# Grid attention: the value products on the tensor array's column halves, with later turns and products

## The reference, cut to what matters

```
s = q @ k.T / 8 (+ a mask: latent tokens see context, and latents at most 128 away)
p = exp(s - m) / (sum(exp(s - m)) + exp(sink - m))      m: a row maximum
o = p @ v;  y = o @ w_o
```

## Time and profile before

| | us |
|---|---|
| median of the runs | 2492.74 |
| the profiled execution | 2491.8 |
| its span | 2490.2 |
| TensorE busy | 2313.0 (93%) |
| VectorE busy | 1218.8 (49%) |
| ScalarE busy | 971.6 (39%) |
| GpSimd busy | 509.9 (20%) |

### The profile page before, as it was taken

How to read it: one execution, slowest core, us unless ns; L and a number is a source line. 1 busy time by engine, 2 the same in 40 slices (tenths; PEclk the granted TensorE clock), 3 DMA queues, 4 the chain that set the end, 5 groups by cost and what they waited for, 6 DMA issues and landing times.

```text
span 2490.2 us, 37770 instructions
## 1 busy us (share of the span) xinstructions
PE 2313.0 (93%) x16663; PEld 2103.8 (84%) x16663; DVE 1218.8 (49%) x1517; ACT 971.6 (39%) x1153; POOL 509.9 (20%) x453
## 2 busy tenths in 40 slices
PE   6999999989999998889999899979999989888998
PEld 6998889879999997567999877867888877667997
DVE  5645566656555553445555355362133264445444
ACT  3433344444433342334444344333222233534442
POOL 2112434312211111220221111012202210230220
PEclk9999999999999998779999999989999999999999
DMA  6555434355555555676554310113332222213551
GB/s 243 176 173 174 140 119 136 124 198 173 183 178 183 182 176 185 212 253 226 181 186 153 110 35 18 35 68 102 101 102 90 97 97 85 68 51 98 179 182 68
DMA packets 205245, 344.72 MB, mean 138 GB/s; under 512 B 8845, under 2 KB 69498, under 8 KB 205082
## 3 DMA queue, kind: packets, MB, share of 16 engines
q1 hardware_dynamic: 205082, 342.31, 41.5%
HBM read 341.24 MB, written 1.05 MB: 137 GB/s over the span
## 4 chain that ended last, share of the span: by engine, by line
PE 77%; DVE 10%; POOL 6%; ACT 4%; issue 3%; SPq 0%; DMA 0%; DVEq 0%; POOLq 0%; ACTq 0%
PE PS L467 74%; PE PS L476 3%; DVE WL L453 3%; POOL small L1504 1%; ACT WH L440 1%; POOL small L1502 1%; POOL TMP L1513 1%; DVE rstd L588 1%; DVE XL L635 1%; DVE TMP L1430 1%; DVE small L1408 0%; DVE XL L1003 0%; DVE al L999 0%; POOL TMP L1514 0%; DVE TMP L1435 0%
## 5 line engine op out<-in xcount | busy, mean ns | idle before, releaser
L453 DVE TENSOR_TENSOR WL<-raw,WH 128x2048 fp32r<-128x2048 f32 (+2 forms) x281 | 651.5, 2331 | 724.5 <-ACT WH L440 724.5
L467 PE MATMUL PS<-XH,WH 128*128 128x256 f32 (+1 forms) x2336 | 699.6, 299 | 40.3 <-issue 15.3
L467 PE MATMUL PS<-XL,WH 128*128 128x256 f32 (+1 forms) x2336 | 693.5, 297 | 0.0
L467 PE MATMUL PS<-XH,WL 128*128 128x256 f32 (+1 forms) x2336 | 693.3, 297 | 0.0
L440 ACT ACTIVATE WH<-raw 128x2048 fp32r<-128x2048 f32 (+2 forms) x281 | 518.8, 1858 | 360.5 <-PE PS L467 360.0
L467 PEld LDWEIGHTS PS<-XH,WH 128*128 128x128 f32 x2336 | 452.1, 194 | 56.8 <-issue 18.5
L467 PEld LDWEIGHTS PS<-XL,WH 128*128 128x128 f32 x2336 | 453.0, 194 | 10.1
L467 PEld LDWEIGHTS PS<-XH,WL 128*128 128x128 f32 x2336 | 452.8, 194 | 10.0
L467 PE MATMUL PS<-WH,XH 128*128 128x256 f32 (+2 forms) x944 | 287.8, 305 | 19.3 <-DVE XL L635 8.3
L467 PE MATMUL PS<-WH,XL 128*128 128x256 f32 (+2 forms) x944 | 279.3, 296 | 0.0
L467 PE MATMUL PS<-WL,XH 128*128 128x256 f32 (+2 forms) x944 | 279.2, 296 | 0.0
(11 more groups left out here) (236 smaller groups left out, 2574.0 us busy)
## 6 DMA issues: line engine op xcount, KB each, us to landing
raw<-in_ffn_w_in SPq DMA_DIRECT2D x88, 1024.0 KB, 5.1
raw<-in_w_mod SPq DMA_DIRECT2D x48, 1024.0 KB, 5.2
raw<-in_ffn_w_out SPq DMA_DIRECT2D x40, 1024.0 KB, 4.9
raw<-in_a_w_in SPq DMA_DIRECT2D x36, 1024.0 KB, 4.9
raw<-in_w_mlp_in SPq DMA_DIRECT2D x32, 1024.0 KB, 5.5
raw<-in_w_mlp_out SPq DMA_DIRECT2D x32, 1024.0 KB, 5.0
raw<-in_gla_w_in SPq DMA_DIRECT2D x12, 1024.0 KB, 5.1
raw<-in_attn_w_qkv SPq DMA_DIRECT2D x6, 1024.0 KB, 5.0
```

The costliest lines, as they stand in the source:

```text
L453: dve.e.tensor_tensor(self.WL[j % NRAW][:, 0:nk * nn], self.raw[j % NRAW][:, 0:nk * nn], wh.bitcast(F32), ALU.subtract).then_inc(*self.lo. ...
L467: return self.pe.e.matmul(out, l, r, start=start, stop=stop, skip_group_check=skip)
```

## The change

The products swap their operands: 64 columns of values are the weights and the turned probabilities stream; the even head goes to PSUM partitions 0 to 63, the odd one to 64 to 127, their matmuls in turn. `cO` then has the channels on the partitions, as the output products want them. The denominators are spread over 64 columns each by ScalarE (`recips`), transposed by TensorE (`sums`) and multiplied in by VectorE (`out`), after ScalarE copied bank 7 (`out`). The sink is no column of the tile any more: its exponential is made once for a group and segment and added to the sums. Score tiles are 6 instead of 4. Probabilities are turned two double steps after their scores, products made three after. On ScalarE the copy of the turned probabilities stands ahead of both exponentials, on VectorE the negation is made once for both heads. The splits for the output products are made in the last group's double steps.

```diff
+        self.cSM += [v(H, 11280, [128, 512]), v(self.tmp_at, 3072, [128, 512]), self.std, self.rstd]
+        self.cO = v(H, 7184, [128, 4096]).rearrange("p (h k t) -> p h k t", h=2, k=KT)
+        self.cRD = v(self.tmp_at, 3584, [128, 512])
...
+        def pv(g, i0):
...
             for k in range(n):
-                m = self.mm(PS[:, 7, o * 256 + hd * 64:o * 256 + hd * 64 + 64], self.cPT[i % 2][:, k * 128:k * 128 + 128], self.cV[:, k, g * 64:g * 64 + 64], k == 0, k == n - 1)
+                for j in range(2):
+                    m = self.mm(PS[64 * j:64 * j + 64, 7, pair * 256 + o * 128:pair * 256 + o * 128 + 128], self.cV[:, k, g * 64:g * 64 + 64], self.cPT[j][:, k * 128:k * 128 + 128], k == 0, k == n - 1, True)
...
+            if i0 % 8 == 6:
+                self.empties([7], (self.evac, ("grid", "o", g, seg)))
+                sums(g, seg)
+
+        def sums(g, seg):
+            nonlocal spare
+            b = spare = self.GRID_SPARE[spare]
+            pe.wait_ge(self.evac, ("grid", "r", g, seg))
+            self.pe_bank(b)
+            for pair in range(2):
+                for o in range(2):
+                    m = self.tr(PS[:, b, pair * 256 + o * 128:pair * 256 + o * 128 + 128], self.cRD[:, 256 * o + 128 * pair:256 * o + 128 * pair + 128])
...
+            self.empties([b], (self.o_done, ("grid", g, seg)))
...
-        for n in range(34):
+        for n in range(35):
             g, p = divmod(n, 8)
             if n < 32:
...
                 scores(g, 2 * p)
                 next(nxt, None)
-            for j in range(2):
-                if n > 1:
-                    g, p = divmod(n - 2, 8)
-                    pv(g, 2 * p + j)
-                if 1 <= n < 33:
-                    g, p = divmod(n - 1, 8)
+            if n > 2:
+                g, p = divmod(n - 3, 8)
+                pv(g, 2 * p)
+            if 2 <= n < 34:
+                g, p = divmod(n - 2, 8)
+                for j in range(2):
                     turn_p(g, 2 * p + j)
-        for h in range(2):
-            self.turn_o_pe(f"go{h}", self.cO[:, 2 * h:2 * h + 2, :], (self.o_done, ("grid", 3, 1)), h)
...
+            if i % 8 == 7:
+                act.wait_ge(self.v_step, ("grid", "sinks", g, seg))
+                act.e.activation(e8, e8, ACT.Exp).then_inc(*self.expd.up(("grid", "sinks", g, seg)))
...
+            if n > 4 and n % 4 == 1:
+                recips(*divmod(n // 4 - 1, 2))
+            if n < 32 and p == 0 and g < 3:
+                nxt = queries(g + 1)
+            if 2 <= n < 34:
+                g1, p1 = divmod(n - 2, 8)
                 turn_p(g1, 2 * p1)
             if n < 32:
+                score(g, 2 * p)
                 score(g, 2 * p + 1)
                 next(nxt, None)
+            if n > 5 and n % 4 == 2:
+                out(*divmod(n // 4 - 1, 2))
+            if 27 <= n < 33:
+                seg, g3 = divmod(n - 27, 3)
+                split(g3, seg)
+            if n == 33:
+                split(3, 0)
+        split(3, 1)
...
+            if n > 6 and n % 4 == 3:
+                out(*divmod(n // 4 - 1, 2))
             if n < 32:
                 score(g, 2 * p)
-                score(g, 2 * p + 1)
                 if g < 3 and p == 0:
                     self.dve_begin()
-            if 1 <= n < 33:
-                g, p = divmod(n - 1, 8)
+            if n and n % 4 == 0:
+                recips(*divmod(n // 4 - 1, 2))
+            if 2 <= n < 34:
+                g, p = divmod(n - 2, 8)
                 turn_p(g, 2 * p + 1)
-            if n > 1:
-                g, p = divmod(n - 2, 8)
-                pv(g, 2 * p + 1)
-        for h in range(2):
-            self.turn_o_dve(f"go{h}", h)
+            if 28 <= n < 34:
+                seg, g3 = divmod(n - 28, 3)
+                split(g3, seg)
+        out(3, 1)
+        split(3, 0)
+        split(3, 1)
...
     def gla_sp(self):
-        sp.wait_ge(self.o_done, ("grid", 3, 1))
+        sp.wait_ge(self.xl, ("go1", 6))
```

More of the change, by code:

```diff
@@ L288, in phase_views @@
         self.cQT = [v(H, 3072 + 1024 * i, [128, 1024]).rearrange("p (a t) -> p a t", a=2) for i in range(2)]
-        self.cSM = [v(H, 5120 + 520 * i, [128, 520]) for i in range(2)]
-        self.cSM += [v(H, 11280, [128, 520]), v(self.tmp_at, 3072, [128, 520])]
+        self.cSM = [v(H, 5120 + 520 * i, [128, 512]) for i in range(2)]
+        self.cSM += [v(H, 11280, [128, 512]), v(self.tmp_at, 3072, [128, 512]), self.std, self.rstd]
         self.cPT = [v(H, 6160 + 512 * i, [128, 512]) for i in range(2)]
-        self.cO = v(H, 7184, [128, 4096]).rearrange("p (b d) -> p b d", b=4)
+        self.cO = v(H, 7184, [128, 4096]).rearrange("p (h k t) -> p h k t", h=2, k=KT)
+        self.cRD = v(self.tmp_at, 3584, [128, 512])
         self.gQ = v(H, 0, [128, 1024]).rearrange("p (h t) -> p h t", h=4)
@@ L2403, in grid_act @@
         KD = TMP[:, 1024:3072].rearrange("p (b g u d) -> p b g u d", b=4, g=4, u=2)
-        nm, dens = self.small[:, 108:112], [self.small[:, 160 + 8 * i:168 + 8 * i] for i in range(2)]
+        nm, dens = [self.small[:, 32 + 8 * i:40 + 8 * i] for i in range(2)], [self.small[:, 160 + 8 * i:168 + 8 * i] for i in range(2)]
+        e8, rd = self.small[:, 48:56], self.small[:, 116:124]
         self.act_begin()
@@ L2464, in grid_act @@
         nxt = iter(())
-        for n in range(34):
+        for n in range(35):
             g, p = divmod(n, 8)
[L2467 to L2470, removed]
-            if 1 <= n < 33:
-                g1, p1 = divmod(n - 1, 8)
+            if n > 4 and n % 4 == 1:
[4 more added lines that the diff above has]
+                g1, p1 = divmod(n - 2, 8)
                 turn_p(g1, 2 * p1)
             if n < 32:
+                score(g, 2 * p)
                 score(g, 2 * p + 1)
                 next(nxt, None)
-        for h in range(2):
-            self.turn_o_act(f"go{h}", h)
-        self.last_products_act("grid", True, 0, 0, [(self.turned, ("go1", "o", 3))])
+            if n > 5 and n % 4 == 2:
[6 more added lines that the diff above has]
+        split(3, 1)
+        self.last_products_act("grid", True, 0, 0, [(self.xl, ("go1", 6)), (self.weighed, ("grid", 3, 15))])
     def grid_dve(self):
@@ L2483, in grid_dve @@
         sk8 = self.small[:, 88:104]
-        mx, nm = self.small[:, 104:108], self.small[:, 108:112]
+        mx, nm = [[self.small[:, at + 8 * i:at + 8 * i + 8] for i in range(2)] for at in (16, 32)]
+        e8 = self.small[:, 48:56]
         dens, rd = [self.small[:, 160 + 8 * i:168 + 8 * i] for i in range(2)], self.small[:, 116:124]
@@ L2517, in turn_p, with recips @@
             dve.e.tensor_copy(self.cPT[1][:, 0:n * 128], PS[:, self.bank_of["grid", "p", g, i], 0:n * 128]).then_inc(*self.emptied.up(("grid", "p", g, i)))
[L2519 to L2523, removed]
-            dve.e.reciprocal(rd, dens[seg]).then_inc(*self.v_step.up(("grid", "recip", g, seg)))
[L2525 to L2530, removed]
+        def recips(g, seg):
+            dve.wait_ge(self.expd, ("grid", "sinks", g, seg))
+            dve.e.tensor_tensor(dens[seg], dens[seg], e8, ALU.add).then_inc(*self.v_step.up(("grid", "sum", g, seg)))
+            dve.wait_ge(self.v_step, ("grid", "sum", g, seg))
+            if g or seg:
+                dve.wait_ge(self.evac, ("grid", "r", g, 0) if seg else ("grid", "r", g - 1, 1))
+            dve.e.reciprocal(rd, dens[seg]).then_inc(*self.v_step.up(("grid", "recip", g, seg)))
@@ L2532, in grid_dve, with out, split @@
+        def out(g, seg):
+            O = self.cO[:, seg, 2 * g:2 * g + 2, :]
+            dve.wait_ge(self.evac, ("grid", "o", g, seg))
+            dve.wait_ge(self.turned, ("grid", "r", g, seg))
+            dve.e.tensor_tensor(O, O, PS[:, self.bank_of["grid", "r", g, seg], :].rearrange("p (k t) -> p k t", k=2), ALU.mult).then_inc(*self.o_done.up(("grid", g, seg)))
+        def split(g, seg):
+            self.split_o_dve(f"go{seg}", g, seg, self.cO[:, seg, 2 * g:2 * g + 2, :])
         self.dve_begin()
-        for n in range(34):
+        for n in range(35):
```

71 lines of the change are left out of this document (42 added, 29 removed).

## The result

The changed kernel takes 2516.18 us (median of 4 executions, 2509.23 to 2516.60) against 2494.86 (4 executions, 2491.65 to 2498.28) of the kernel before on the same chip: ratio 1.0079, 95% interval 1.0055 to 1.0102. It is slower, as forecast, but by 21 us where 12 were forecast. The time is 0.2 us above 2516, the upper end of the wider range; the kernel before, measured beside it, was itself 2.1 us above the 2492.74 from which the forecast counted, and the difference of 21.3 is less than the 23 that the range allows. In a second set of runs the kernel took 2510.41 us, ratio 1.0053 (1.0036 to 1.0071). The profiled execution took 2516.35, its span is 2515.0, 24.8 more than before.

A forecast was written before the change was run, and what follows sets the result against it. TensorE's order was taken to bound the kernel. Order +8 and clock +5 make +13 on the profiled 2491.8, 0.9 below the median: 2505 us; own range 2495 to 2513, wider 2487 to 2516.

The forecast's parts named there:

- order of the work: Grid attention from first scores to first output product: steps and waits, without new clock falls, add 8 us.
- clock in loop and tail: Grid attention: three of five new TensorE idles are followed by a clock fall, adding 5 us (bounds 0 and +17).
- 16 products in halves: Value products of a latent double step, run in column halves, take 1.06 us instead of 1.68.
- first wait of p7: In groups 0 to 2 the first query transpose waits 1.9 us for VectorE's `out` to read the denominators' bank.
- second wait of p7: TensorE's second turn waits for ScalarE's query copy to free the first query transpose's bank, near 3.1 us.
- p7: Last of the eight double steps of a head group: 9.26 us instead of 5.96 in groups 0 to 2.
- wait of p1: In groups 1 and 2 TensorE's products wait 2.9 us for VectorE's copy of the turned probabilities.
- p1: Second of the eight double steps of a head group: 8.7 us in groups 1 and 2, 5.95 before.
- rival 4: Products in column halves halve with nothing lost on switching, 20 us gained: 2473 us, chance 0.03.
- rival 1: Neither the wait in p1 nor the new ones in p7 bind: -8, 2485 us, chance 0.17.
- rival 2: Only one wait binds, that of p1 is absent and the clock does not fall: +2, 2495 us, chance 0.12.
- rival 3: In the grid attention the clock falls after every new idle and for longer: +8 and +17, 2517 us, chance 0.08.

The follow-up runs named there:

- experiment 5: Changed kernel with 165 extra transposes that nobody reads, filling TensorE's waits, order otherwise untouched; 2502.98 us, ratio 1.0049.
- experiment 8: Kernel before the change, with ScalarE's query copies in p7 moved ahead of the turned probabilities; 2486.30 us, ratio 0.9991.
- experiment 1: Changed kernel with VectorE's weight-block subtraction moved behind its copy of turned probabilities in the first double step of groups 0 to 2; 2503.39 us, ratio 1.0045.
- experiment 2: Changed kernel with ScalarE's query copies in p7 moved ahead of the turned probabilities and exponentials; 2495.37 us, ratio 1.0019.
- experiment 3: Changed kernel with ScalarE's copy of bank 7 (`out`) moved ahead of the turned probabilities and exponentials; 2497.06 us, ratio 1.0026.
- experiment 7: Changed kernel with ScalarE's query copies in p7, bank 7 copy and first double step's weight split ahead of the turned copy; 2476.13 us, ratio 0.9928.
- experiment 10: Changed kernel run once more, word for word; 2510.41 us, ratio 1.0053.

## Why the prediction was right or wrong

The direction and the mechanism of the two waits were right; the size of the clock's term was not. The +24.8 of the profiled execution consist of three parts:

| part | forecast | measured | from |
|---|---|---|---|
| order of the work | +8 | +6.0 | 153.53 (exp. 5) - 147.5 (exp. 8) |
| clock in loop and tail | +5 | +9.1 | 164.77 - 153.53, less before's 2.2 |
| clock behind the loop | 0 | +9.8 | 920.96 - 911.21 |

The prediction set its group 3 against today's with the fall of the clock in the tail in it; by that accounting the first two rows are +4.9 and +10.2. They sum to the +15.1 of loop and tail either way. That the forecast's +13 is so near to +15.1 is in part luck: by its own accounting the order was put 3 us too high and the clock 5 us too low.

**The order, step by step.** Read at full clock (experiment 5):

| | forecast | measured |
|---|---|---|
| 16 products in halves | 1.06 | 1.02 |
| first wait of p7 | 1.9 | 1.89 |
| second wait of p7 | 3.1 | 2.76 |
| p7 | 9.26 | 9.01 |
| wait of p1 | 2.9 | 2.64 |
| p1 | 8.7 | 8.44 |
| p0, p2, p3 | 5.8, 5.8, 5.0 | 5.75, 5.75, 4.87 |
| p4, p5, p6 | 2.8, 2.8, 3.3 | 2.71, 2.71, 3.14 |
| groups 1 and 2 | 43.5 | 42.4 |
| group 0 against before | +0.3 | +0.35 |
| p3, p5 of group 3 | 3.5, 3.3 | 3.37, 2.75 |
| tail | 12.9 | 12.77 |

Both new waits of the forecast are shown, and each by the edit that takes it away (experiments 1, 2, 3 and 7). What was off in the order is small and all to one side: the wait of p1 was sized 0.26 too long, the second one of p7 0.34, p5 of group 3 0.55. The prediction's steps of group 3 add up to 22.2, not to the 21.9 that it gives; measured are 20.86 at full clock. The run of 16 products came out as worked from the dilated attention's rows, 1.02 against 1.06; that they halve to 0.84 with nothing lost (rival 4) is out, as are rivals 1 and 2, since both waits bind.

**The term that was mis-sized** is the clock's: "Near the middle of the nearest rows I take three: +5." All five waits were followed by half clock, in both profiled executions of the changed kernel. Against the steps at full clock the five stretches cost 1.4 to 3.2 us each and 10.7 together in the first profile, and 9.1 in the second (162.59 - 153.53); three times 1.7 was the sum. Behind the number stands a misread row: "the wait of 2.1 us in p7" that kept the clock. The 2.1 run from the end of the first turn to the second one and hold the second head's products; TensorE was idle for 1.13 of them (the row under experiment 8), so no row showed that an idle of 2 us keeps the clock. The changed kernel has 1.89 and 2.76 within 7.3 us (1457.13 to 1464.45). A wait of 1.89 without the second one was followed by half clock in two groups of three (experiment 2). The fall in the tail, priced at 1.7 from its length, cost 1.1 (experiment 8). So the case was nearer to rival 3, "the clock falls every time and for longer", in its number of falls, and between the two in its price. That 2516.18 lies at that rival's 2517 is chance: its +8 and +17 in the loop measured +4.9 and +10.2, and 9.8 came behind the loop, where it had nothing.

**What the forecast did not have at all** is how far executions of the same code differ behind the loop. Thirteen profiles show that part at 909.5 to 921.0 us, the changed kernel at both ends. The Trainium skill ("TensorE: Matmul & The Clock Gate", What's actually happening) says that the same kernel starts with a different number of slow matmuls from run to run; the two profiles of one kernel show such a difference behind the loop too, 11.5 us in 920, with a clock of 0.95 in one and 0.96 in the other. In the second set the change costs 14.4 us (0.53%), about what the loop alone gives (+12.9 in that profile, +15.1 in the first). In the first set it costs 21.3, 6 more than the loop gives; whether the changed kernel has its long executions behind the loop more often than the kernel before, the traces do not tell. Why executions of one kernel lie 8 us apart, as in experiments 5 and 8, was not tried and stays open.

No cost of SP's later wait shows, as forecast: with it the part behind takes 909.5 and 911.5 us (experiments 10 and 7), without it 911.2.

## What to carry to other kernels

Swapping operands and using column halves made the products as short as the rows said (1.02 us for 16 instead of 1.68), and the gain was lost because three small pieces of work on ScalarE and VectorE, which are busy for less than half of the time, stood in the wrong place in their engine's order: the two copies of p7, and the weight's split or its subtraction. Moving these alone turned +0.5% to +0.8% into -0.5% to -0.7%. When a change makes one engine's steps shorter or later, list for each other engine what stands ahead of the piece that the first one waits for, and put work that waits for nothing ahead of work that waits. Count the clock with every wait of TensorE: here half as much again as the wait itself was lost behind it.

## What the runs showed of the hardware that was not expected

In the changed kernel the waits of 1.89 to 2.76 us were followed by a granted clock of 1.2 GHz, in all five places. Two windows, around the end of p7 of group 0 and of group 2:

```profile
1460.00:1470.00 10.00, 7.24 (x45) 5.87 (x45) 2.31 (x10) 3.07 (x8) 0.00 (x0) 0.70 0.00 0
...
1550.00:1560.00 10.00, 5.98 (x38) 4.16 (x40) 3.19 (x9) 3.46 (x9) 0.01 (x1) 0.64 0.01 2
```

The length of a wait alone does not decide it. In experiment 2 the wait of p1 has the same length as in the changed kernel, and the 16 products behind it run at full clock:

```profile
1473.15 1.09 PE L468 MATMUL PS<-al,al 128*64 128x128 f32 x16 [2.63 <-ACT al L2490]
```

In the changed kernel, where the two waits of p7 come shortly before, they took up to 1.98 (1525.42, above). So a wait that keeps the clock in one order of the work may lose it in another, which is why its price could not be read from single waits of the kernel before. Filling the waits with 165 transposes of no use, at no cost in the order, gave 9 to 11 us of loop and tail back (experiment 5): this stretch was shorter with TensorE kept busy for nothing than with TensorE waiting. The medians of the whole kernels (ratios 1.0049, and 1.0079 and 1.0053) do not tell the two apart with certainty. Removing the waits was better still, by 18.7 us in the loop (153.53 to 134.83).
